# A two-block transformer kernel: the first slot alone, equal tile offsets, norms and bias turns moved, a shorter end

## The chip, the cores and the metric
The kernel runs on one core of one Trainium2 chip. The metric is the device time of one execution in microseconds, as the median of several runs. Engines: TensorE (PE; its weight loads are PEld), VectorE (DVE), ScalarE (ACT), GpSimd (POOL) and SyncE (SP, which only issues DMAs here; ScalarE issues some too).

## The reference, cut to what matters
Input x has 512 tokens of width 1024. Everything is fp32.

Block one: h = rms_norm(x); one projection gives the inputs of four mixers of width 256: a short convolution, a sparse attention of three parts (compressed tokens, selected blocks, a window; `ksw`, `nq0`, `nq1`, `kvc`), a latent attention with rotary parts (`cq`, `ckv`, called mla), and a stick-breaking attention (`sq0` to `sk1`, called sb). Each mixer's output is normed (`y`), then x += y @ w_out, then a feed-forward of width 4096 with a squared relu.

Block two: retention, gated linear attention and sliding-window attention, each projected and gated, merged, projected, normed and added to x; then

```python
h = rmsnorm(x, norm_ffn_pre)
f = (silu(h @ ffn_w_gate) * (h @ ffn_w_up)) @ ffn_w_down
x = x + rmsnorm(f, norm_ffn_post)
```

## The kernel before
**Layout.** Activations lie transposed: 8 chunks (KD) of 128 features by 512 tokens (T). A projection of 128 output features takes one weight slot (128 x 1024). Each fp32 product is made of three fp32r matmuls (`mm3`, L700): with w and x split in a high and a low part, w_hi x_hi + w_hi x_lo + w_lo x_hi. So a projection (`fm`, L803) is 24 matmuls of 512 columns into one of 8 PSUM banks.

**Weight slots.** SyncE loads slots in order into 3 raw buffers (L2066 to L2082). GpSimd makes the high part (L2054) and the low part by a subtraction (L2056), into 3 buffers each, as these are freed by TensorE. From `fg` 0,3 on ScalarE makes the high part. The slots of the compression weights (`cmp`, steps `cmp_up`) are not split; they have three buffers of their own.

**Order.** `plan()` (L71) writes out one list, ORDER, by hand. Each engine walks the same list and does its own part of each step, in this order, with semaphores between. `together` and `quarters` (L82, L91) cut projections in pieces by chunk (`fmk`, L768); `weave` (L119) spreads filler steps among the steps of an attention: `att_scores` (product, row maximum on VectorE L1822, Exp on ScalarE L1380), `att_norm` (L1840 to L1844), `att_turn` (transposes L962, copied out by ScalarE L1392 as att_pt), `att_pv`. A stick-breaking step `sb_scores` makes two score matmuls, then per head Abs, Exp, Ln on ScalarE (L1418 to L1420) and one operation on VectorE (L1894); `sb_exp` sums these by matmuls and takes Exp (L1428).

**Banks.** `take` (L674) hands out the bank that was filled longest ago and waits until it has been evacuated.

**Norms.** A norm step squares chunks on ScalarE (`sq`, L1157), adds them on VectorE (sq_sum, L1502), sums over partitions with a matmul by ones (`ms`, L717), and makes rstd by Ln and Exp on ScalarE (L1170, L1173). n1, the first one, is applied behind the projection (as r_h, when banks are evacuated: L1586 to L1594), so matmuls run on x times the norm's weights: `u` makes its high part on ScalarE (L1213) and low part on VectorE (L1542). The projection that follows y_out is made from four mixers' norms, the last y3 (L203 to L204).

**The start** (L152 to L166): per chunk `u` and `sq`; TensorE waits for both first slots (`kvc`, `ksw`, L773) and runs chunks 0 to 6 of both, the matmul of n1, and chunk 7; then `nq0`, the compression windows (`cmp_x`, L1722 to L1727), the bias tables (L750, copied at L1532), the norm and scaling of ksw (L1734), `nq1` and so on. At these steps ScalarE issues DMAs for constants.

**The bias turns** (L912): 32 matmuls of 31 columns turn the compressed bias (cb_t) by `flip`, in one block, ahead of `cmp_down`. `cmp_scores` has a softmax on VectorE behind it (L1784 to L1805), `cmp_turn` transposes the result.

**The end.** `down2` (L841, 22 hidden chunks in two halves, slots without a gap) makes f: half 0 is copied from the banks to SBUF (L1711), half 1 is added (L1709). Then the norm `fpost`, and per chunk two VectorE operations: f times weight times rstd (L1507), and x plus this (L2021); SyncE writes each chunk out (L2094).

**SBUF.** Tiles are laid out one behind the other (L363 on). Counted from the start of the partition, x_sb, h, w_hi_t, w_lo_t, u2_hi, hid and most of block two start at 128 modulo 256 bytes; ones, ident, sq, sq_sum, rstd_t, tmp, att_l_t, att_pt and u2_lo05 at 0; the constants of block one behind `gates` at 32 or 64. The low parts of norm2's x are u2_lo05 (chunks 0 to 5) and u2_lo67 (6, 7; at 128): both are called u_lo in the trace.

Of the kernel before, what the change touches and what calls it, by code (L numbers as in the profile page):

```python
# [70 lines left out]
def plan():  # L71
# [47 lines left out]
    def weave(main, filler):  # L119

        n = 0
        for i, step in enumerate(main):
            put(step)
            while n < len(filler) and n * len(main) < (i + 1) * len(filler):
                put(filler[n])
                n += 1
        for step in filler[n:]:
            put(step)
# [32 lines left out]
    run([("sq", "ksw", 0), ("cmp_x", 0), F("nq0"), ("cmp_x", 1), ("bias_tables", 0), ("norm", "ksw"),  # L161
         ("nsa_apply", "ksw"), F("nq1"), ("sq", "nq0", 0), U(0, 0), F("cq0"), ("sq", "nq1", 0), ("norm", "nq0"),
         ("nsa_apply", "nq0"), U(0, 1), F("cqr"), ("norm", "nq1"), ("nsa_apply", "nq1"), ("sq", "cq", 0),
# [4 lines left out]
    for h in range(NH):  # L168
# [3 lines left out]
    run([("cmp_bias", 0), ("cmp_down", 0), ("sq", "kcmp", 0), ("mla_v", 0)] + filler[:5] + [("norm", "kcmp"), ("cmp_apply", 0)] +  # L172
        filler[5:10] + [("cmp_scores", 0)] + filler[10:16] + [("cmp_turn", 0)])
    filler = filler[16:]
# [19 lines left out]
    for n in range(4):  # L194
# [9 lines left out]
        [part(3, 6), ("norm", ("y", 3)), ("y_out", 3), part(6, KD)])  # L204
# [72 lines left out]
    for c in range(KD):  # L277
        order.append(("residual", "fpost", c))
# [32 lines left out]
o_ready m_ready gla_v gla_s gla_kd gla_st gla_a gla_done gla_t prod gate_s merged merged_hl q_s swa_s ft lo_t table""".split()  # L311
# [32 lines left out]
def _program(ctx, nc, a, known):  # L344
# [22 lines left out]
    par = sb("par", [P, -(-NPCOL // 32) * 32])  # L367
    ones = sb("ones", [P, P])
# [9 lines left out]
    small = sb("small", [P, 4, 8])  # L378
    r_col = small[:, :, 7]
# [12 lines left out]
    v1 = sa("v1", [P, NT, 396])  # L392
    gates = sa("gates", [P, NT, 12])
    rb = sa("rb", [N_BUCKETS + 1, NH])
# [15 lines left out]
    conv_t = sa("conv_t", [P, 2, 2 + T])  # L410
# [29 lines left out]
    cmp_bias = sn("cmp_bias_t", [P, NT, NH, N_CMP])  # L440
    cmp_t = sn("cmp_t", [P, 256])
# [66 lines left out]
    f_acc = merged  # L508
    hid2 = [si("hid2_hi", [P, HALF2, T], F32R), si("hid2_lo", [P, HALF2, T], F32R)]
    sig2, sig_g = si("sig2", [P, 2, T]), si("sig_g", [P, 2, T])  # L510
    inner.close()
    area.close()

# [157 lines left out]
    def _(pe):  # L671
# [28 lines left out]
        def mm3(out, wh, wl, xh, xl, start, stop):  # L700

            mm(out, wh, xh, start, False)
            mm(out, wh, xl, False, False)
            return mm(out, wl, xh, False, stop)
# [12 lines left out]
        def ms(key, n_src):  # L717
            srcs, parts, cols, one, *_ = norms[key]
            out = take(("ms", key))
# [24 lines left out]
        for step in ORDER:  # L744
            stage = step[0]
            if stage == "bias_tables":
# [3 lines left out]
                for n, (c0, w) in enumerate(TAB):  # L750
                    out = take(("tab", n))
                    fill(("tab", n), mm(out[0:NH, 0:w], rb[:], onehot[:, c0:c0 + w], True, True))
# [15 lines left out]
            elif stage == "fmk":  # L768

                _, names, src, k0, k1 = step  # L770
                for name in names:
                    if k0 == 0:
                        slot_ready(SLOTS[name][0])  # L773
                        take(name)
# [4 lines left out]
                for k, some in blocks:  # L779
                    fresh = src == "h" and ("h_ready", seen_h, k) not in chunks_seen  # L780
                    if fresh:
# [4 lines left out]
                    for name in some:  # L786
# [8 lines left out]
                    if fresh:  # L795
# [45 lines left out]
            elif stage == "down":  # L841
# [4 lines left out]
                out = take(nm)  # L846
                for k in range(nk):
# [4 lines left out]
                    if o == 0:  # L852
# [3 lines left out]
                               k == 0, k == nk - 1)  # L856
                    if k == nk - 1:
# [54 lines left out]
            elif stage == "cmp_bias":  # L912

                out = take("cmp_bias")
                for qt in range(NT):
                    for h in range(NH):
                        last = mm(out[:, (qt * NH + h) * N_CMP:(qt * NH + h + 1) * N_CMP],
# [1376 lines left out]
```

## Time and profile before

| what | value |
|---|---|
| median of 3 runs | 1884.86 us (1883.58 to 1885.2) |
| the profiled execution | 1885.97 us |
| its span, first to last instruction | 1884.1 us |
| mean granted TensorE clock | 0.988 |
| busy: PE, PEld, DVE, ACT, POOL | 1820.3, 1433.4, 834.9, 504.8, 944.6 us |
| HBM read, written | 158.1, 2.1 MB |

Times of rows are microseconds from the span's start. Matmuls are pipelined: one of 512 columns is shown with 0.39 us, but the next begins 0.227 us behind it. The granted clock is a share of 2.4 GHz; 0.50 is 1.2 GHz.

### The profile page before, as it was taken

The numbers are of one execution on the slowest core, as the hardware profiler recorded it, in microseconds if no ns is written. First come the engines' busy times: TensorE is split into PE (matmuls) and PEld (weight loads), VectorE is DVE, ScalarE is ACT, GpSimd is POOL, SyncE is SP. The second block draws the span as 40 slices with busy tenths as digits, with TensorE's granted clock in tenths as the row PEclk, the third lists the DMA queues.
The fourth block names the chain that finished last, engine by engine and source line by source line (L and its number), as shares of the span: only waits on it lengthen the run. The fifth ranks groups of instructions, "written<-read, shape, count | busy, mean of one in ns | idle before, by whom it ended". The sixth has DMA issues, their size and how long they took to land.

```text
span 1884.1 us, 22044 instructions
## 1 busy us (share of the span) xinstructions
PE 1820.3 (97%) x8468; PEld 1433.4 (76%) x8468; DVE 834.9 (44%) x1386; ACT 504.8 (27%) x1003; POOL 944.6 (50%) x510
## 2 busy tenths in 40 slices
PE   7999989999999999999999999999999999999996
PEld 5785556888888887777887888677778778888885
DVE  6418754532022232435103574666655675315433
ACT  3115664221012001222003232555400232222221
POOL 5343131766666665454665555443466554444541
PEclk9999999999999999999999999999999999999998
DMA  5620100332232223122232222212122223223231
GB/s 179 199 80 26 47 23 34 101 101 97 93 101 90 100 91 111 67 79 79 97 101 79 67 79 76 67 63 68 60 90 97 89 79 100 93 98 101 90 101 56
DMA packets 46728, 162.54 MB, mean 86 GB/s; under 512 B 5392, under 2 KB 6736, under 8 KB 46241
## 3 DMA queue, kind: packets, MB, share of 16 engines
q1 hardware_dynamic: 43088, 154.52, 24.3%
q10 hardware_dynamic: 3537, 6.61, 1.2%
q8 instruction: 69, 1.13, 0.2%
q14 instruction: 34, 0.28, 0.0%
HBM read 158.13 MB, written 2.12 MB: 85 GB/s over the span
## 4 chain that ended last, share of the span: by engine, by line
PE 88%; DVE 6%; ACT 3%; issue 2%; POOL 1%; DMA 0%; ACTq 0%; DVEq 0%; POOLq 0%
PE bank L698 87%; PE bank L962 1%; DVE att_l_t L1822 1%; POOL w_lo_t L2056 1%; DVE o_hi L1485 1%; DVE tmp L1507 0%; ACT att_l_t L1380 0%; DVE o_lo L1486 0%; DVE att_l_t L1842 0%; ACT rstd_t L1170 0%; ACT sq L1157 0%; ACT sb_e L1419 0%; ACT rstd_t L1173 0%; ACT att_pt L1392 0%; DMA w_raw<-in_w 0%
## 5 line engine op out<-in xcount | busy, mean ns | idle before, releaser
L2056 POOL TENSOR_TENSOR w_lo_t<-w_raw,w_hi_t 128x1024 fp32r<-128x1024 f32 x276 | 691.7, 2506 | 188.2 <-ACT w_hi_t L1196 170.1
L2054 POOL TENSOR_SCALAR w_hi_t<-w_raw 128x1024 fp32r<-128x1024 f32 x216 | 234.9, 1088 | 683.7 <-PE bank L698 653.3
L698 PE MATMUL bank<-h_hi,w_hi_t 128*128 128x512 f32 x1088 | 445.3, 409 | 23.6 <-POOL w_lo_t L2056 13.9
L698 PE MATMUL bank<-h_hi,w_lo_t 128*128 128x512 f32 x1088 | 428.4, 394 | 0.0
L698 PE MATMUL bank<-h_lo,w_hi_t 128*128 128x512 f32 x1088 | 421.2, 394 | 0.5 <-DVE h_lo L1575 0.5
L698 PEld LDWEIGHTS bank<-h_hi,w_hi_t 128*128 128x128 f32 x1088 | 207.0, 190 | 87.6 <-issue 39.3
L698 PEld LDWEIGHTS bank<-h_lo,w_hi_t 128*128 128x128 f32 x1088 | 206.6, 190 | 47.0 <-issue 2.6
L698 PEld LDWEIGHTS bank<-h_hi,w_lo_t 128*128 128x128 f32 x1088 | 206.9, 190 | 42.4 <-issue 1.0
L698 PE MATMUL bank<-hid_hi,w_lo_t 128*128 128x512 f32 x432 | 168.2, 389 | 0.0
L698 PE MATMUL bank<-hid_lo,w_hi_t 128*128 128x512 f32 x432 | 168.2, 389 | 0.0
L698 PE MATMUL bank<-hid_hi,w_hi_t 128*128 128x512 f32 x432 | 168.2, 389 | 0.0
L1196 ACT ACTIVATE w_hi_t<-w_raw 128x1024 fp32r<-128x1024 f32 x60 | 63.6, 1060 | 219.8 <-PE bank L698 219.8
L698 PE MATMUL bank<-u_lo,w_hi_t 128*128 128x512 f32 x256 | 100.8, 394 | 0.0
L698 PE MATMUL bank<-u_hi,w_hi_t 128*128 128x512 f32 x256 | 100.1, 391 | 0.0
L698 PE MATMUL bank<-u_hi,w_lo_t 128*128 128x512 f32 x256 | 99.5, 389 | 0.0
L698 PEld LDWEIGHTS bank<-hid_hi,w_lo_t 128*128 128x128 f32 x432 | 81.1, 188 | 16.9
L698 PEld LDWEIGHTS bank<-hid_hi,w_hi_t 128*128 128x128 f32 x432 | 81.1, 188 | 16.8
L698 PEld LDWEIGHTS bank<-hid_lo,w_hi_t 128*128 128x128 f32 x432 | 81.1, 188 | 16.7
L698 PE MATMUL bank<-o_hi,w_hi_t 128*128 128x512 f32 x192 | 78.3, 408 | 2.1 <-DVE o_lo L1486 2.1
L1380 ACT ACTIVATE att_l_t<-att_l_t,small 128x256 f32<-128x256 f32 (+3 forms) x112 | 57.3, 512 | 78.3 <-DVE small L1826 47.1
L1261 ACT ACTIVATE r<-r 128x512 f32<-128x512 f32 x32 | 20.3, 633 | 216.2 <-DVE r L1641 216.2
L1641 DVE SCALAR_TENSOR_TENSOR r<-bank,r_h 128x512 f32<-128x512 f32 x32 | 22.1, 692 | 124.6 <-PE bank L698 120.2
(276 smaller groups left out, 2619.8 us busy)
## 6 DMA issues: line engine op xcount, KB each, us to landing
w_raw<-in_w SPq DMA_DIRECT2D x276, 512.0 KB, 3.2
y<-in_w SPq DMA_DIRECT2D x6, 512.0 KB, 6.2
x_sb<-in_x SPq DMA_DIRECT2D x4, 512.0 KB, 7.6
x_sb<-in_x ACTq DMA_DIRECT2D x2, 1024.0 KB, 5.4
out_y<-x_sb SPq DMA_DIRECT2D x8, 256.0 KB, 2.0
u_raw<-in_w SPq DMA_DIRECT2D x2, 512.0 KB, 6.0
toep<-table ACTq DMA_DIRECT2D x4, 256.0 KB
decay<-in_decay SPq DMA_DIRECT2D x1, 1024.0 KB, 4.9
```

The costliest lines, as they stand in the source:

```text
L698: return pe.matmul(out, lhs, rhs, start=start, stop=stop, **kw)
L962: last = pe.transpose(out[:, b * P:(b + 1) * P], att_l[:, att_at[u] % 4, b * P:(b + 1) * P], ident[:])
L1196: act.activation(w_hi[:, RING[i]], w_raw[:, n % RAW], ACT.Copy).then_inc(*did("wa_hi", i))
L1261: chain(act.activation(r1[:, n % 2], r1[:, n % 2], ACT.Square))
L1380: act.activation(L, L, ACT.Exp, bias=sm[:, 1:2], accum_out=sm[:, 2:3]).then_inc(*did("att_exp", u))
L1485: chain(dve.tensor_copy(hi, t))
L1641: dve.scalar_tensor_tensor(out=r1[:, n % 2], in0=ps(name)[:], scalar=0.0, in1=r_h[:], op0=ALU.max, op1=ALU.mult).then_inc(*release(name))
L1822: dve.tensor_tensor_reduce(L, ps(("sc", u))[:, 0:A["w"]], A["bias"], 1.0, -3.0e38, ALU.add, ALU.max, sm[:, 0:1]).then_inc(*release(("sc", u)))
L2054: pool.tensor_scalar(hi, raw, 1.0, 0.0, ALU.mult, ALU.add).then_inc(*did("w_hi", i))
L2056: pool.tensor_tensor(lo, raw, hi.bitcast(F32), ALU.subtract).then_inc(*did("w_lo", i))
```

## The change
What it does, in the order of the list:

- The first slot alone. `u` runs three chunks ahead of `sq`. `kvc` takes the high parts of chunks 0 to 3 (w_hi and w_lo by x_hi) when its own slot is ready, then `ksw` the same, then both the low parts of these chunks, then chunks 4 to 7.
- The norm n1 stands behind the first quarter of `nq0`, and evacuations of `kvc` and `ksw` behind it; the rest of `nq0` before the square of ksw. `cmp` quarter 0,1 goes ahead of the norm of nq0.
- The bias turns are cut by head in four pieces of 8 matmuls; `cmp_down` comes before them, and `mla_qk` of head 1 before `cmp_scores`.
- `weave` holds an `sb_scores` filler back while the step just put is `att_scores` or `att_norm`, once a turn has been made. Worked through, this moves three such fillers in the latent attention behind the next `att_turn` (sb_scores (0,1), (0,0) and (1,3)); nothing in the other two attentions.
- The norm of y3 comes after chunk 3 of the pieces of `wout`, not after 5.
- Chunk 7 of `down2` keeps one bank over both halves, so VectorE does nothing for it; its square is taken from the bank in two halves of 256 columns, and the norm `fpost` is made in two halves.
- The last adds (`last_add`): for chunks 0 to 3 VectorE only multiplies; TensorE adds x and the product in a bank (by ident), ScalarE copies it to x_sb. Chunks 4 to 7 stay on VectorE. Output order 0, 4, 1, 5, 2, 3, 6, 7.
- Tile offsets: `small` moves ahead of `ones`, v1, gates, rb, conv_t get padding, and 16 elements go ahead of cmp_t, so all start at 128 modulo 256.

```diff
-    for c in range(KD):
-        run([("u", "n1", c), ("sq", "n1", c)])
+    for c in range(KD + 3):
+        run([("u", "n1", c)] * (c < KD) + [("sq", "n1", c - 3)] * (c >= 3))
     part, ends = together(("kvc", "ksw"))
-    run([part(0, KD - 1), ("norm", "n1"), part(KD - 1, KD)] + ends)
+    run([("fmk", ("kvc",), "h", 0, 4, "hi"), ("fmk", ("ksw",), "h", 0, 4, "hi"),
+         ("fmk", ("kvc", "ksw"), "h", 0, 4, "lo"), part(4, KD)])
...
-    run([("sq", "ksw", 0), ("cmp_x", 0), F("nq0"), ("cmp_x", 1), ("bias_tables", 0), ("norm", "ksw"),
-         ("nsa_apply", "ksw"), F("nq1"), ("sq", "nq0", 0), U(0, 0), F("cq0"), ("sq", "nq1", 0), ("norm", "nq0"),
-         ("nsa_apply", "nq0"), U(0, 1), F("cqr"), ...
+    nq0 = quarters("nq0")
+    run(nq0[:1] + [("norm", "n1")] + ends + nq0[1:] + [("sq", "ksw", 0), ("cmp_x", 0), ("cmp_x", 1), ("bias_tables", 0), ("norm", "ksw"),
+         ("nsa_apply", "ksw"), F("nq1"), ("sq", "nq0", 0), U(0, 0), F("cq0"), ("sq", "nq1", 0), U(0, 1),
+         ("norm", "nq0"), ("nsa_apply", "nq0"), F("cqr"), ...
...
-    run([("cmp_bias", 0), ("cmp_down", 0), ("sq", "kcmp", 0), ("mla_v", 0)] + filler[:5] + [("norm", "kcmp"), ("cmp_apply", 0)] +
-        filler[5:10] + [("cmp_scores", 0)] + filler[10:16] + [("cmp_turn", 0)])
+    run([("cmp_down", 0), ("sq", "kcmp", 0), ("cmp_bias", 0), ("mla_v", 0)] + filler[:3] + [("norm", "kcmp"),
+        ("cmp_apply", 0), ("cmp_bias", 1)] + filler[3:4] + [("cmp_bias", 2)] + filler[4:8] + [("cmp_bias", 3)] +
+        filler[8:10] + filler[11:13] + [("cmp_scores", 0)] + filler[13:15] + filler[10:11] + [("cmp_turn", 0)])
...
             while n < len(filler) and n * len(main) < (i + 1) * len(filler):
+                if turned and not callable(filler[n]) and filler[n][0] == "sb_scores" and step[0] in ("att_scores", "att_norm"):
+                    break
...
-        [part(3, 6), ("norm", ("y", 3)), ("y_out", 3), part(6, KD)])
+        [part(3, 4), ("norm", ("y", 3)), part(4, 6), ("y_out", 3), part(6, KD)])
...
+            if (key, c) == ("fpost", KD - 1):
+                act.wait_ge(*full(last_f))
+                sq_free(key, c)
+                for hf in range(2):
+                    act.activation(sq[:, sq_use[(key, c)] % 2, halves_t[hf]], ps(last_f)[:, halves_t[hf]], ACT.Square)\
+                       .then_inc(*did("sq_s", key, c, hf))
+                return
...
+            elif stage == "last_add":
+                r = rstd("fpost")
+                for c in range(KD):
+                    t = last_t[c] if c < N_PE else tmp[:, c % 2]
+                    f = f_acc[:, c] if c < KD - 1 else ps(last_f)[:]
...
+                    for part in halves_t if c == 0 else [slice(0, T)]:
+                        if c == 0:
+                            own("rstd", "fpost", halves_t.index(part))
+                        ins = dve.scalar_tensor_tensor(out=t[:, part], in0=f[:, part], scalar=col("fpost", c),
+                                                       in1=r[:, part], op0=ALU.mult, op1=ALU.mult)
+                    if c < N_PE:
+                        ins.then_inc(*did("last_t", c))
+                    else:
+                        chain(ins)
+                        dve.tensor_tensor(x_sb[:, c], x_sb[:, c], t, ALU.add).then_inc(*did("x_ready", "fpost", c))
```

## Rows read from the trace of the kernel before
**Rows 1.** The page: busy us of each engine, share of the span, instructions.
```profile
PE 1820.3 (97%) x8468; PEld 1433.4 (76%) x8468; DVE 834.9 (44%) x1386; ACT 504.8 (27%) x1003; POOL 944.6 (50%) x510
```
**Rows 2.** Stretches: length, busy and count of each engine, granted clock, DMA, GB/s.
```profile
52.20:55.50 3.30, 3.30 (x7) 1.89 (x7) 0.13 (x1) 1.94 (x3) 1.49 (x1) 0.50 0.45 124
127.30:134.10 6.80, 6.80 (x28) 6.29 (x28) 1.10 (x2) 0.61 (x3) 1.49 (x1) 0.50 0.22 77
...
263.90:270.60 6.70, 6.62 (x15) 4.48 (x16) 3.36 (x12) 3.53 (x9) 0.00 (x0) 0.50 0.00 0
321.90:325.20 3.30, 3.30 (x9) 2.55 (x9) 1.37 (x3) 1.24 (x2) 2.15 (x2) 0.50 0.00 0
```
**Rows 3.** Waits of TensorE: for whom, us in total, times, longest.
```profile
PE bank L698 <- ACT att_pt L1392: 8.2, 4, 4.5
...
PE bank L698 <- ACT sq L1157: 4.4, 4, 1.9
```
**Rows 4.** Timeline of the start: start, us, engine, line, operation [idle before].
```profile
6.09 2.34 POOL L2056 TENSOR_TENSOR w_lo_t<-w_raw,w_hi_t 128x1024 fp32r<-128x1024 f32 x1
8.13 0.72 ACT L1213 ACTIVATE h_hi<-x_sb,par 128x512 fp32r<-128x512 f32 x1 [6.14 <-DMA x_sb<-in_x]
...
8.97 3.76 DVE L1542 SCALAR_TENSOR_TENSOR h_lo<-x_sb,par,h_hi 128x512 fp32r<-128x512 f32 x2 [7.25 <-ACT h_hi L1213]
...
9.52 2.66 POOL L2056 TENSOR_TENSOR w_lo_t<-w_raw,w_hi_t 128x1024 fp32r<-128x1024 f32 x1
...
12.44 0.77 PE L698 MATMUL bank<-h_hi,w_hi_t 128*128 128x512 f32 x1 [12.44 <-POOL w_lo_t L2056]
...
14.71 2.87 DVE L1502 TENSOR_TENSOR sq_sum<-sq_sum,sq 128x512 f32<-128x512 f32 x1
...
27.35 0.63 ACT L1173 ACTIVATE r_h<-r_h 128x512 f32<-128x512 f32 x1
```
**Rows 5.** The chain that ended last, 36 to 57: start, us, what.
```profile
44.56 2.55 DVE x_sb L1734
...
51.23 0.64 ACT sq L1157
```
**Rows 6.** Groups of TensorE from 125 to 130.3: busy us, mean ns.
```profile
L698 PE MATMUL bank<-flip,cb_t 31*128 31x31 f32 x32 | 5.1, 321 | 0.0
```
**Rows 7.** Timeline of TensorE around the first attention pair.
```profile
155.39 1.07 PE L698 MATMUL bank<-sq,ones 96*96 96x512 f32 x2 [1.28 <-ACT sq L1157]
158.43 0.93 PE L962 MATMUL bank<-ident,att_l_t 128*128 128x128 f32 x2 [1.97 <-DVE att_l_t L1842]
```
**Rows 8.** Timeline around the longest wait: ScalarE's Abs, the norm of y1.
```profile
258.73 0.57 ACT L1418 ACTIVATE sb_e<-bank 128x512 f32<-128x512 f32 x1
...
272.12 1.13 PE L698 MATMUL bank<-sq_sum,ones 128*128 128x512 f32 x2
```
**Rows 9.** Timeline of the norm of y3.
```profile
311.49 0.69 DVE L1502 TENSOR_TENSOR sq_sum<-sq 128x512 f32<-128x512 f32 x1 [8.15 <-ACT sq L1157]
...
315.91 1.02 PE L698 MATMUL bank<-sq_sum,ones 128*128 128x512 f32 x2
...
319.69 0.50 PE L698 MATMUL bank<-h_hi,w_hi_t 128*128 128x512 f32 x1 [2.76 <-DVE h_hi L1571]
...
320.95 0.49 PE L698 MATMUL bank<-h_lo,w_hi_t 128*128 128x512 f32 x1 [0.53 <-DVE h_lo L1575]
```
**Rows 10.** Tiles u_lo and hid_lo: duration ns min/median/max, first and last start.
```profile
L698 PE MATMUL bank<-u_lo,w_hi_t x256: 389/395/396, 354.3 to 617.6; 128*128 128x512 f32 x128
...
L698 PE MATMUL bank<-hid_lo,w_hi_t x432: 388/389/390, 443.6 to 1865.7; 128*128 128x512 f32 x144
```
**Rows 11.** Timeline of the end.
```profile
1866.40 0.69 DVE L1709 TENSOR_TENSOR merged_t<-bank,merged_t 128x512 f32<-128x512 f32 x1 [5.40 <-PE bank L698]
...
1870.45 0.75 DVE L1507 SCALAR_TENSOR_TENSOR tmp<-merged_t,par,rstd_t 128x512 f32<-128x512 f32 x1 [3.36 <-ACT rstd_t L1173]
...
1880.95 0.69 DVE L2021 TENSOR_TENSOR x_sb<-x_sb,tmp 128x512 f32<-128x512 f32 x1
```

More of the change, by code:

```diff
@@ L276, in plan @@
     order.append(("norm", "fpost"))
-    for c in range(KD):
-        order.append(("residual", "fpost", c))
+    order.append(("last_add", "fpost"))
     return order, slots
@@ L718, in ms @@
             srcs, parts, cols, one, *_ = norms[key]
+            if key == "fpost":
+                outs = [take(("ms", key, hf))[:, 0:T // 2] for hf in range(2)]
+                pe.wait_ge(*after("sq_v", key, KD - 2))
+                for hf in range(2):
+                    mm(outs[hf], one[:], sq_sum[:, halves_t[hf]], True, False)
+                for hf in range(2):
+                    pe.wait_ge(*after("sq_s", key, KD - 1, hf))
+                    fill(("ms", key, hf), mm(outs[hf], one[:], sq[:, sq_use[(key, KD - 1)] % 2, halves_t[hf]],
+                                             False, True))
+                return
             out = take(("ms", key))
@@ L785, in _ @@
                     wsl = slice(k * P, (k + 1) * P)
-                    for name in some:
+                    for name in some if only != ["lo"] else ():
                         i = SLOTS[name][0]
@@ L845, in _ @@
                 nm = (name[0], name[1], o)
-                out = take(nm)
+                both = name[0] == "down2" and o == KD - 1
+                if nm == last_f:
+                    tenants[nm] = tenants[("down2", 0, o)]
+                    out = ps(nm)
+                else:
+                    out = take(nm)
                 for k in range(nk):
@@ L1162, in norm @@
             functions("exp_ln")
+            if key == "fpost":
+                act.wait_ge(*after("rstd_used", ring_order[ring_at[key] - 3]))
+                for hf in range(2):
+                    r_half = rstd(key)[:, halves_t[hf]]
+                    act.wait_ge(*full(("ms", key, hf)))
+                    act.activation(r_half, ps(("ms", key, hf))[:, 0:T // 2], ACT.Ln, scale=scale,
+                                   bias=small[:, EPS_COL[eps], 6:7]).then_inc(*release(("ms", key, hf)))
+                    act.wait_ge(*evacuated(("ms", key, hf)))
+                    act.activation(r_half, r_half, ACT.Exp, scale=-0.5).then_inc(*did("rstd", key, hf))
+                return
             act.wait_ge(*full(("ms", key)))
@@ L1458, in _ @@
                 act.activation(g_ed[:], g_ed[:], ACT.Exp).then_inc(*did("gla_s", "ed", h))
+            elif stage == "last_add":
+                for c in range(N_PE):
+                    act.wait_ge(*full(("last", c)))
+                    act.activation(x_sb[:, c], ps(("last", c))[:], ACT.Copy).then_inc(*did("last_x", c))
             elif stage == "gla_turn":
@@ L1703, in _ @@
                     hidden_low(name[1], HALF1 - 1)
+                if name[0] == "down2" and o == KD - 1:
+                    continue
                 dve.wait_ge(*full(nm))
```

101 lines of the change are left out of this document (65 added, 36 removed).

## The prediction
> **What bounds the kernel now.** I read the page first: TensorE is busy for 97% of the span, the next engine for 50% [rows 1]. The reader should see two things: nothing but TensorE's own instructions can be worth much in the long stages, and an edit that removes no matmul can only win back TensorE's idle time, its time at the lower clock, the few ns by which a matmul is dearer than its neighbours, and what lies behind the last matmul. Then the view by stretches, cut where the granted clock falls: in five short stretches (four stand here) the clock is 0.50, the lower of its two levels, 1.2 instead of 2.4 GHz [rows 2]. TensorE lost half of each, if it had work. Before the first it had stood still for 1.9 us (the longest of its waits on a square) and before the third for 4.5 us (the longest on att_pt) [rows 3]; before the second it ran 31-column matmuls. Then the timelines and the chain around the stalls, part by part.
>
> **Part 1, the start.** Today the first projection matmul starts at 12.44, when the low part of the second weight slot is done (9.52 + 2.66 = 12.18), though the first slot was done at 6.09 + 2.34 = 8.43 and the first high part of x at 8.13 + 0.72 = 8.85 [rows 4]. The change lets `kvc` run alone on high parts of chunks 0 to 3. It starts at about 8.9, 3.5 us earlier. Its 8 matmuls, at some 0.45 us each at the lower clock (7 in 3.30 us [rows 2]), last until 12.5, just when `ksw` is ready: no new wait there. ScalarE now issues the high parts ahead of the squares (0.7 us each), so chunks 1 to 3 come in time. The low parts don't gain: VectorE's run from 8.97 for 3.76 us for two, and a sum took 2.87 us where 0.69 is usual, both beside GpSimd's subtraction [rows 4]. I put the last low part at about 21.7 instead of 23.3, the two projections done at 23.3, a quarter of `nq0` done at 24.7, and the norm's matmuls then, so r_h appears at about 28.0, as today (27.35 + 0.63) [rows 4]. But TensorE has only 18 matmuls of `nq0` behind it instead of 30 (6 of the pair, 24 of `nq0`): it is 3.3 us ahead.
>
> What it meets next is the chain from r_h over VectorE (three copies, two window builds, a memset, four table copies), ScalarE and back, which today ends with the square at 51.9 [rows 5], TensorE 1.9 us idle before it, and the clock low for 3.4 us after [rows 2, 3]. In this chain the change takes the 0.7 us copy of `nq0` off the path (it now fits in a wait for a DMA), and the weight slots are freed earlier, so GpSimd's subtractions move away from VectorE's two-input operations: the key scaling's first half took 2.55 us beside one [rows 5], the second 0.75 (47.13 to 47.88). Worked through, the square of `nq0` comes at about 47.7 instead of 51.23. TensorE, 5.1 us ahead by then (3.3, plus 1.8 of a `cmp` quarter that the new order puts before the norm), reaches the norm at about 48.3 and need not wait. So the part gives the lead, the wait and half of the cold stretch: 3.3 + 1.9 + 1.7 = **6.9 us** (the 1.8 are only moved). Bounds: if the chain moves by nothing beyond 0.7 us and the cold stretch stays, 3.5; if all is as good as its order, 8.5. SyncE's queue keeps its order (slot numbers don't change); its loads wait for freed slots, all earlier, and ScalarE's DMA issues keep theirs.
>
> **Part 2, bias turns in pieces.** The 32 small matmuls take 5.1 us in one block [rows 6], and inside it the clock falls for 6.8 us [rows 2]. Four pieces of eight between projections and full-width products leave no such block. If the cold stretch goes, 3.4 us come back. Against that: three more changes between kinds of matmul at about 0.2 us; and the scores now come after `mla_qk` of head 1, so that TensorE meets `cmp_turn` some 2.6 us before VectorE's softmax chain (5.3 us from scores to probabilities) is through. Today it pays there later: 1.28 us for a square and 1.97 us for the first weights [rows 7]. This stage's exit is set by VectorE, whose list loses only the copy and the rotation before the first scores. I take **0.5 us**; between 2.5 lost (cold stretch stays, wait is new) and 3 gained.
>
> **Part 3, the stick-breaking scores behind the turn.** TensorE's waits on att_pt are 8.2 us in 4, the longest 4.5 [rows 3]. The timeline shows why: ScalarE takes up the two heads' Abs, Exp, Ln at 258.7 [rows 8] and reaches the transposed weights only behind them and a norm; TensorE goes on at 264, cold [rows 2]. The new rule in `weave` moves three of the scores steps behind `att_turn`: the copy then comes at about 258.7. TensorE's next block (2.6 us) is filled in, but ScalarE's work in front of the norm of y1 (3.7 us of Abs, Exp, Ln, a norm of 1.3, two squares, a copy, two exponentials) is not less: that norm moves from 272.12 [rows 8] to about 268. So 4 us, plus 1 us at the first moved step (a wait of 1.2 us of the same kind), and nothing at the third, where TensorE doesn't wait: **5 us**. Bounds 1.5 (ScalarE gives all back) and 7.
>
> **Part 4, the norm of y3** goes two chunks earlier. Today the norm's matmuls run at 315.91; then TensorE waits 2.76 us for its first high part and 0.53 for the low part [rows 9], then runs 3.3 us cold [rows 2]. After the change 18 matmuls (4.1 us) lie behind the norm's matmuls, where from their start to the first high part 3.7 us are needed (319.63 - 315.91): covered. Left are 0.5 us ahead of the norm (the sum is ready at 311.49 + 0.69 = 312.2, TensorE is there at 315.9 - 4.1 - 0.1 = 311.7) and 0.2 for the last low part. 3.3 - 0.7 + 1.7 (half of the cold stretch) = **4.3 us**; bounds 3.0 and 4.8.
>
> **Part 5, offsets.** `small` moves ahead of `ones`, and tiles of the first area are padded, so that all start at the same remainder of 256 bytes as x and the weights. One tile shows what this may be worth: u_lo's matmuls have a median of 395 ns against 389 at best and for the hidden ones [rows 10]. Six of its eight chunks lie in `u2_lo05`, 128 bytes off in this measure, two in `u2_lo67`, which isn't, and the cheap ones are the latter. Start to start it is about 7 ns, for 192 matmuls 1.3 us. VectorE's two-input operations take 0.69 us on tiles of either kind (sq_sum, merged) [rows 9, 11]. I take **1.3 us**; bounds 0 (the cause is another) and 3, if matmuls beside such tiles in the attention stages gain too.
> The Trainium skill (SBUF — State Buffer, "Who interferes with whom") gives a single rule: only the port pair shared by VectorE and GpSimd causes contention. It knows no cost of an offset for TensorE. By that rule the part is worth 0 and the sum is 1.3 us smaller; the row of u_lo speaks against it.
>
> **Part 6, the end.** From the last projection (1866.40) to the first output step are 4.05 us: add, square, ones product, Ln, Exp; then VectorE makes eight pairs of 0.75 and 0.69, 11.2 us, and the last DMA ends the span 2.5 us later [rows 11]. The change accumulates both halves of chunk 7 in one bank, so the add goes; squares read the bank, in halves; rstd comes in halves, the first after about 2.3 us, the second after 3.1. Then VectorE has chunk 0 in two halves, three single multiplies (2.2 us) and four pairs with 1.39 each (5.55): last output at 3.5 + 2.2 + 5.55 = 11.25 us behind the projection, today 15.24 (1881.64). TensorE's ones and adds of x (0.86 us a product, twice that when cold) and ScalarE's four copies are done by about 8 us; SyncE's order 0, 4, 1, 5, 2, 3, 6, 7 queues none behind a later one. **4.0 us**; bounds 3.3 and 4.5. The bank held from `down2` half 0 to the end leaves seven, which a projection of 5.4 us each doesn't need; without that cover each late bank would cost the 0.7 us of a copy.
>
> **Sum:** 6.9 + 0.5 + 5 + 4.3 + 1.3 + 4.0 = 22.0 us. The profiled execution took 1885.97 us (span 1884.1 and 1.9 around it), the median of the runs is 1.1 lower. 1885.97 - 22.0 = 1864.0; against the median 1862.9. I say 1863.2, between the two.
>
> **Rivals.**
> (a) *The stalls move.* TensorE's lead is eaten by the chains of VectorE and ScalarE, which no part shortens: 3.5 (part 1), -1 (part 2), 1.5, 3.3, 0, 4.0 = 11.3 us, 1873.6. For it: from 162 to 325 TensorE often waits on them [rows 3, 7]. Against: the order, not the amount, made the largest waits. 25%.
> (b) *The clock gives more.* All cold stretches of block one go, and the offsets help the attention stages: 8.5 + 3 + 7 + 4.8 + 3 + 4.3 = 30.6, about 1854.5. For it: dense work stands where idle was. 10%.
> (c) *Slower: equal offsets collide.* If the slow remainder is not the odd one but the one that two engines share, the moved tiles (tmp, sq, att) now share it with x and the weights. Price: up to 7 ns on each of some 6,600 projection matmuls, 46 us, so 1863 + 46 = 1909. It decides from 4 ns on (26 us: the 22 gained and 4 more). Against: the hidden ones run at 389 beside VectorE's work on tiles of the same remainder [rows 10]. 2%.
> (d) *It doesn't do what it says:* the offsets do nothing, and the cold stretches around the bias turns and the norm of y3 stay: 1.3 + 3.4 + 1.7 = 6.4 us less, though the other parts hold: about 1869.5. 10%.
> The forecast has 53%.
>
> **Numbers.** The range from 1857 to 1873.5 leaves out most of (b), (c) and the worse half of (a). About 0.2%, 3.8 us, is what a measurement of this kernel can tell from no change; part 6 alone nearly makes that, so faster 0.96, same 0.02, slower 0.02.
>
> **What would show it.** First matmul near 9; r_h near 28; clock full at 52 to 55, at 127 less 7, and around 312 to 318; no wait over 1.5 us on att_pt, with the copies ahead of the Abs; no wait on h_hi at y3; u_lo's median 389 or 390; last DMA issued 11.3 us behind the last projection. It is wrong if TensorE waits long for the square of `nq0`, for `cmp_p`, or for a new ScalarE step in the attention stage, or if projection matmuls are no longer 227 ns apart.

## The result, and the profile after

The changed kernel takes **1874.95 us** (median of 4 runs, 1873.66 to 1876.29), the kernel before beside it 1884.55: a ratio of 0.995, interval 0.9934 to 0.9966, so 9.6 us faster where some 21 were forecast, and above the range. The sign was right; the size was the size of rival (a), 1873.6, though not by its parts.

The page's first part, as [rows 1]; the span is 1874.5 us, 9.6 less than before:
```profile
PE 1826.0 (97%) x8488; PEld 1433.5 (76%) x8488; DVE 826.7 (44%) x1381; ACT 507.0 (27%) x1010; POOL 943.6 (50%) x510
```
TensorE is busy for 5.7 us longer than before: behind the last projection 9.0 instead of 2.1 us, most of it the 7.3 us of identity products of the new end, and ahead of it 1.2 us less. What is missing is seen in the stretches (columns as in [rows 2]):
```profile
134.00:146.10 12.10, 9.90 (x59) 6.43 (x58) 7.54 (x15) 3.15 (x5) 3.40 (x2) 1.00 0.15 51
146.10:159.70 13.60, 10.16 (x36) 5.88 (x36) 9.21 (x36) 5.73 (x18) 0.00 (x0) 0.50 0.00 0
159.70:163.00 3.30, 3.30 (x20) 2.01 (x16) 1.40 (x5) 0.54 (x3) 0.70 (x1) 1.00 0.00 0
268.90:272.40 3.50, 3.50 (x5) 1.25 (x4) 3.43 (x7) 1.32 (x2) 0.00 (x0) 0.51 0.00 0
702.40:709.30 6.90, 6.04 (x14) 4.78 (x15) 6.87 (x14) 0.00 (x0) 0.00 (x0) 0.51 0.33 131
```
The low stretches at 52, in the bias turns and at the norm of y3 [rows 2] are gone, as forecast. In their place stands one of 13.7 us around the first attention steps, where the kernel before had 3.4; TensorE is busy for 10.16 us of it, half of them lost to the clock. With a longer stretch at 702 (6.8 for 3.4) and a new one of 3.4 at 1371, the low stretches ahead of the end sum up to 34 us in both kernels: none of the clock that I counted as won was won in the sum. (Up to 400 us they went from 23.8 to 17.1; behind that they grew from 10.2 to 17.0.)

To find where the time went, take a mark that both traces have: the start of ScalarE's Ln in each norm. The lead of the changed kernel over the one before, in us, by single profiled executions (mk and mq are the latent attention's keys and queries by head, y the mixers' norms, n2 the norm behind the mixers, pre the one at the end of block one, ret 0 the first of retention, fpre the one ahead of the last feed-forward):

| kernel | ckv | mk 0 | mq 1 | mq 3 | y0 | y1 | y2 | n2 | pre | ret 0 | fpre | time, median |
|---|---|---|---|---|---|---|---|---|---|---|---|---|
| (time in before) | 79.59 | 143.67 | 167.34 | 220.04 | 262.34 | 273.28 | 294.00 | 361.26 | 707.90 | 777.76 | 1529.08 | 1884.55 |
| after | 6.6 | 12.0 | 2.8 | 2.3 | -0.8 | 4.0 | 2.3 | 6.2 | 7.5 | 6.2 | 5.5 | 1874.95 |
| e1 the same | 5.9 | 11.2 | 2.6 | 2.1 | -1.0 | 3.9 | 2.2 | 6.0 | 7.2 | 6.0 | 6.5 | 1875.02 |
| e2 part 2 undone | 6.9 | 6.5 | 6.4 | 6.3 | 2.7 | 6.7 | 5.9 | 9.7 | 11.0 | 10.9 | 10.1 | 1872.24 |
| e3 weave undone | 6.6 | 11.9 | 3.6 | 3.1 | 3.6 | 5.2 | 5.2 | 9.0 | 10.2 | 10.2 | 9.9 | 1872.55 |
| e4 y3 undone | 5.8 | 11.1 | 2.7 | 2.1 | -1.0 | 3.6 | 2.2 | 2.2 | 3.5 | 2.6 | 3.3 | 1876.52 |
| e5 both of e2, e3 | 6.6 | 7.8 | 7.4 | 7.4 | 7.3 | 8.9 | 8.8 | 12.6 | 13.9 | 13.9 | 14.0 | 1870.82 |
| e6 pieces, old order | 7.0 | 12.2 | 9.0 | 8.9 | 5.3 | 9.2 | 8.4 | 12.2 | 13.5 | 13.5 | 14.0 | 1871.0 |
| e7 two fillers | 6.7 | 12.0 | 5.3 | 4.6 | -0.6 | 3.3 | 2.5 | 6.3 | 7.6 | 9.2 | 9.5 | 1874.68 |
| e8 offsets undone | 6.6 | 12.2 | 4.0 | 2.9 | -0.2 | 3.7 | 2.9 | 6.7 | 6.7 | 6.7 | 6.8 | 1875.12 |
| e9 e6 without rule | 7.0 | 12.3 | 8.7 | 8.8 | 8.8 | 9.8 | 9.8 | 13.6 | 14.9 | 14.8 | 14.3 | 1868.18 |
| e10 e9, one step held | 6.5 | 11.8 | 8.2 | 8.2 | 3.9 | 8.2 | 7.0 | 10.9 | 12.2 | 11.1 | 11.7 | 1870.11 |
| e11 e9 without part 1 | 0.2 | 5.5 | 1.4 | 1.5 | 1.5 | 2.5 | 2.5 | 6.3 | 7.6 | 7.6 | 7.2 | 1873.17 |
| e13 held behind att_pv | 7.0 | 12.3 | 7.9 | 8.0 | 7.2 | 12.4 | 9.2 | 13.0 | 14.3 | 14.3 | 14.9 | 1867.83 |
| e14 the same, three | 7.0 | 12.3 | 8.7 | 8.7 | 9.3 | 14.6 | 14.2 | 17.8 | 19.1 | 19.0 | 19.5 | 1862.69 |
| e15 e9 again | 5.5 | 10.8 | 6.1 | 5.5 | 5.5 | 6.5 | 6.5 | 10.3 | 11.6 | 11.6 | 11.1 | 1870.05 |

The row "after" has the account: part 1 gives 6.6, part 2 takes 4.4 (to mq 3; the 12 at mk 0 is only its new place, and mq 1 and y0 don't stand at the same point of the order in all kernels either, while mq 3, y1, y2 and what follows do), part 3 nothing (2.3 to 2.3), part 4 3.8, part 5 1.3, two longer low-clock stretches take 1.9, and the end, 4.1 more, brings it to 9.6. The same program's profile differs by 1.5 us at ckv and 3.3 at mq 3 from another execution's (e9 and e15), because its low stretches differ; so a difference under some 3 us between two rows is read only where it is the step from one mark to the next, and one under 2 us between medians of different series not at all (e9 and e15 are 1.87 apart).

**Part 1** is as forecast. The first matmul, forecast for 8.9, and the square of nq0, forecast for 47.7 (TensorE had no wait of 1.9 us left and the clock stayed up):
```profile
8.71 0.77 PE L709 MATMUL bank<-h_hi,w_hi_t 128*128 128x512 f32 x1 [8.71 <-ACT h_hi L1274]
...
48.57 0.63 ACT L1208 ACTIVATE sq<-x_sb 128x512 f32<-128x512 f32 x1 [6.11 <-issue]
```

**Part 2.** TensorE's waits in the changed kernel, from 134 to 167 us (for whom, us in total, times, longest). Before, from 140 to 174, there were 1.28 and 1.97 [rows 7]:
```profile
PE bank L993 <- DVE att_l_t L1911: 3.3, 1, 3.3
PE bank L971 <- DVE cmp_p L1874: 2.4, 1, 2.4
```
And what VectorE does there, from the timeline of the changed kernel:
```profile
141.09 0.74 DVE L1860 TENSOR_TENSOR cmp_p<-bank,cmp_bias_t 128x248 f32<-128x248 f32 x2 [2.07 <-PE bank L709]
...
145.54 0.67 DVE L1874 TENSOR_TENSOR cmp_p<-cmp_p,cmp_s_t 128x496 f32<-128x496 f32 x1
...
149.06 0.68 DVE L1943 TENSOR_TENSOR mq<-mq,rope_c 96x512 f32<-96x512 f32 x1
...
151.41 0.35 DVE L1911 TENSOR_SCALAR att_l_t<-att_l_t,small,gates_t 128x128 f32<-128x128 f32 x1
```
VectorE now stands idle for 2.07 us until the later scores are there, and the rest of its chain, down to the first weights at 151.4, comes behind them.

**Part 3.** TensorE's waits on att_pt fell from 8.2 to 4.4 us and the norm of y1 came at 268.07, as forecast, but a new wait stands before it:
```profile
268.07 1.19 PE L709 MATMUL bank<-sq_sum,ones 128*128 128x512 f32 x2 [2.18 <-DVE sq_sum L1567]
```
ScalarE's waits from 217.78 to 291.66 us, which in the kernel before (220.04 to 294.0) were 6.8 us in 5 on the same tile:
```profile
ACT att_l_t L1441 <- DVE small L1898: 11.7, 7, 2.7
ACT att_pt L1453 <- PE bank L709: 11.2, 6, 3.8
```

**Part 4.** The wait of 2.76 on the high part [rows 9] and its cold stretch are gone. One wait of another kind came, for a weight slot of GpSimd, which TensorE now reaches 4 us sooner:
```profile
320.41 0.50 PE L709 MATMUL bank<-h_hi,w_hi_t 128*128 128x512 f32 x1 [0.99 <-POOL w_lo_t L2142]
```

**Part 5.** u_lo's matmuls, as [rows 10]:
```profile
L709 PE MATMUL bank<-u_lo,w_hi_t x256: 387/389/396, 348.2 to 610.2; 128*128 128x512 f32 x128
```

**Part 6.** The end, as [rows 11]: squares of the bank, Ln of the first half, first output step and last. The last ends at 1872.04, 11.2 us behind the last projection's matmul (1860.47 + 0.39); forecast were 11.25:
```profile
1860.89 0.66 ACT L1199 ACTIVATE sq<-bank 128x256 f32<-128x256 f32 x2 [6.12 <-PE bank L709]
...
1862.25 0.47 ACT L1219 ACTIVATE rstd_t<-bank,small 128x256 f32<-128x256 f32 x1 [0.70 <-PE bank L709]
...
1863.20 0.49 DVE L2088 SCALAR_TENSOR_TENSOR sig<-merged_t,par,rstd_t 128x256 f32<-128x256 f32 x1 [7.70 <-ACT rstd_t L1222]
...
1871.35 0.69 DVE L2094 TENSOR_TENSOR x_sb<-x_sb,tmp 128x512 f32<-128x512 f32 x1
```

### The profile page after: what moved, and what is told of

Read it like the earlier page. It is cut to its first block, busy times and chain, and to the rows that moved or that the text cites. A ratio compares the mean times of both kernels' runs of the same rounds, so it can differ in the third digit from the quotient of the medians.

```text
span 1874.5 us, 22078 instructions
## 1 busy us (share of the span) xinstructions
PE 1826.0 (97%) x8488; PEld 1433.5 (76%) x8488; DVE 826.7 (44%) x1381; ACT 507.0 (27%) x1010; POOL 943.6 (50%) x510
## 4 chain that ended last, share of the span: by engine, by line
PE 89%; DVE 6%; ACT 3%; issue 1%; POOL 1%; DMA 1%; ACTq 0%; SPq 0%; DVEq 0%; POOLq 0%
PE bank L709 87%; PE bank L993 1%; DVE att_l_t L1911 1%; DVE att_l_t L1891 1%; DVE o_hi L1550 0%; POOL w_lo_t L2142 0%; ACT sq L1208 0%; DVE o_lo L1551 0%; DMA x_sb<-in_x 0%; ACT att_l_t L1441 0%; DVE h_lo L1607 0%; ACT sb_e L1480 0%; ACT att_pt L1453 0%; DVE att_l_t L1913 0%; ACT h_hi L1274 0%
```

## The experiments

The theories that the runs tell apart: **A**, parts 2 and 3 cost time, each by itself, and the others hold; its rivals are that an accident of the clock did it, that a chain of VectorE or ScalarE takes back any lead, or that another part failed. Each kernel was timed 4 to 11 times beside the kernel before, in four series (e1 to e4, e5 to e8, e9 to e12, e13 to e15), in which the kernel before took 1883.1 to 1883.8.

**e1: nothing edited.**

> The changed kernel once more, nothing edited, to have it beside the three kernels that follow and to see a second profile. Theory A (its low-clock stretches belong to the order of its instructions): the long one of 13.7 us from 146.1 to 159.7 comes again within 1 us of the same place, and the median is 1875.0 +/- 1. Rival R (where the clock falls is an accident of one execution): this stretch is missing or as short as 3.4 us, and the span differs by some 4 us from the first profile.

1875.02 us (0.9954, 0.9942 to 0.9967). The long stretch came again, but from 149.7, 3.6 us behind its first place where within 1 was expected, and 10.2 us long, so that both end at 159.8 or 159.9; another of 3.4 came at 33.7, where the first profile had none. So the place belongs to the order; the length partly to the execution. All six profiles with the new order of scores (after, e1, e3, e4, e7, e8) have 10.2 or 13.7 us here, all eleven with the old order (before among them) 3.4 or 6.8.

**e2: part 2 undone.**
```
+run([("cmp_bias", h) for h in range(NH)] + [("cmp_down", 0), ("sq", "kcmp", 0), ("mla_v", 0)] + filler[:5] +
+    [("norm", "kcmp"), ("cmp_apply", 0)] + filler[5:10] + [("cmp_scores", 0)] + filler[10:16] + [("cmp_turn", 0)])
+filler = filler[16:]
```

> The changed kernel with the first block's old order: bias turns in one row ahead of the down product, scores before head 1's keys and queries. Theory A (part 2 costs what the stages between 134 and 167 lost: 6.6 us of lead at the turn of cmp_p, 2.8 us after the first attention steps): about 4 us faster than the changed kernel, 1871 us, with the low-clock stretch between 146 and 160 no longer than 7 us, and one of some 7 us inside the bias turns about 6 us earlier than in the kernel before, near 121. Rival B (the lead is lost there whatever the order, because VectorE's chain from the scores to the first weights sets the end of the stage): within 1 us of the changed kernel, 1875, with the milestone behind the first attention steps where the changed kernel has it, at 164.6.

1872.24 us, 2.8 less than e1; by the marks 4.2 at mq 3 and 3.7 at fpre. The cold bias turns are back and yet it is the faster one:
```profile
121.00:127.80 6.80, 6.80 (x27) 6.20 (x27) 1.10 (x2) 1.02 (x3) 1.27 (x1) 0.50 0.22 77
151.70:155.10 3.40, 3.17 (x8) 2.11 (x8) 2.24 (x13) 2.82 (x9) 0.00 (x0) 0.50 0.00 0
```
Part 2 costs 2.8 to 4.2 us. Rival B, that the lead goes there in any order, falls.

**e3: the rule in `weave` undone.**
```
-if turned and not callable(filler[n]) and filler[n][0] == "sb_scores" and step[0] in ("att_scores", "att_norm"):
-    break
```

> The changed kernel without the rule that holds sb_scores back behind a turn. Theory A (part 3 only moves the stall, because ScalarE's list up to the norm of y2 is as long as before): the norm of y1 comes some 4 us later, at about 273, but the norm of y2 stays within 1 us of 291.7 and the time within 1 us of the changed kernel, 1875. Rival B (part 3 has its 5 us, and something else lost them): 1878.5 to 1880.

1872.55 us, 2.5 less than e1; both expectations missed. The stall of 4.5 us on att_pt is back, and y2 is 3.0 us earlier. So part 3 doesn't move its gain, it costs. (Of the 3.0, 1.0 stands at mq 3 already, ahead of the first moved step: from mq 3 to y2 this kernel gains 2.1 us, the changed one 0.1.)

**e4: the norm of y3 where it was.** `[part(3, 6), ("norm", ("y", 3)), ("y_out", 3), part(6, KD)]`

> The changed kernel with the norm of y3 where it was, behind six chunks of the last three projections. Theory A (part 4 is worth what the milestones behind it show, 3.8 us): 1878.8 us, with TensorE waiting 2.8 us for the first high part again. Rival B (it is worth its wait alone and the rest was the accident of the clock there): 1877.3.

1876.52 us, 1.5 more than e1 and less than either expected, though the marks part by 3.8 at n2 and 3.2 at fpre. The wait of 2.75 us and a stretch of 3.4 at 320.0 are back. The step from y2 to n2 is 3.6 to 3.8 us in all 14 profiles with the part and 0.0 in the three without it (before, e4, e12); the median shows less of it than this, and why, the runs don't say.

**e5: parts 2 and 3 undone together** (e2's and e3's edits).

> The changed kernel with the first block's old order and without the weave rule, parts 1, 4, 5 and 6 kept. Theory A (each of the two parts costs by itself, part 2 2.8 us and part 3 2.5 us by the medians of the runs so far): the sum of both, 1869.7 us, with the norm of y2 7.3 to 9.4 us earlier than in the kernel before. Rival B (the two share one stall, so that either undoing is enough): no better than the better of them, 1872.

1870.82 us (1867.72 to 1872.27), 4.2 less than e1, where the sum of both would be 5.3 and one alone 2.8: a little nearer the sum. By the marks it is the sum (6.6 at y2, of 3.7 and 3.0), but its profiled execution, 1867.78, was 3.0 below its median.

**e6: the pieces kept, the old order of scores and rotation.**
```
-    filler[8:10] + filler[11:13] + [("cmp_scores", 0)] + filler[13:15] + filler[10:11] + [("cmp_turn", 0)])
-filler = filler[15:]
+    filler[8:10] + [("cmp_scores", 0)] + filler[10:16] + [("cmp_turn", 0)])
+filler = filler[16:]
```

> The changed kernel with its bias turns in pieces, but the scores again before head 1's keys and queries and its rotation before the turn of cmp_p; weave rule kept. Theory A1 (what costs in part 2 is the new order, which brings TensorE to cmp_turn and to the first weights before VectorE's chain; the pieces are harmless or help): at or below the run with part 2 wholly undone, 1869 to 1872.5 us, with no wait over 1 us before cmp_turn. Rival A2 (the pieces are what costs; VectorE or ScalarE gets the bias table or the slots too late): 1875 us, as the changed kernel.

1871.0 us, 4.0 below e1. This splits part 2: pieces with the old order lead by 8.9 at mq 3, the block with the old order by 6.3 (e2; 7.4 in e5, whose stretch in the block was 3.4 us instead of 6.8), pieces with the new order by 2.1. By these rows alone the pieces would be worth +1.5 to 2.6 us and the new order -6.8; but this profile is of the fastest of six executions, 3.2 below their median. The step from ckv to mq 3 over all profiles says it better: pieces with the old order 0.1 to 1.9 us in seven (e6, e9, e10, e11, e13, e14, e15; mean 1.3), the block with the old order -0.6 to 0.8 in four (before, e2, e5, e12; mean 0.0), pieces with the new order -3.5 to -4.4 in five (after, e1, e3, e4, e8; mean -3.8). So the new order costs **some 5 us** (4.0 by e6's median beside e1's), clear of the spread, and the pieces bring **about 1.3**, which is not. From 121 to 134, through the last three of the pieces (the first is at 119, the clock full there too), the granted clock is full:
```profile
121.00:134.00 13.00, 13.00 (x60) 8.72 (x59) 3.10 (x6) 4.77 (x9) 1.20 (x1) 1.00 0.14 45
```

**e7: two quarters of a projection into the two waits.** One quarter before `cmp_turn`, the next ahead of head 1's rotation (`filler[13:15] + filler[18:19] + filler[10:11]`, then `filler[19:20] + filler[15:18] + filler[20:]`).

> The changed kernel with two more quarters of the conv projection in the two waits of part 2: one ahead of cmp_turn, the next ahead of head 1's rotation (which then no longer stands before the first weights in VectorE's queue). Theory A1 (TensorE waits there because its order has nothing to do; work moved in is work gained): the wait of 2.4 us before cmp_turn goes, the one of 3.3 before the first weights falls to under 2, the clock does not stay low for 10 us or more, and the time is 1870 to 1872 us. Rival B (VectorE's chain sets the exit of the stage; filling in only moves the waits behind it): within 1 us of the changed kernel, 1875.

1874.68 us: Rival B by the time. The waits did shrink, 5.6 us to 4.2 in five, but TensorE turned the first weights at 150.96 (151.81 in after), and the low stretch is again 10.2 us. The profile leads by 4.6 at mq 3, 2.3 more than after, and has 2.5 at y2, as after; between them stands a low stretch of 3.4 us more, at 254.2. In the old order the first weights are turned at 149.34 (e9), because VectorE has the scores 2.9 us sooner (0.4 of it that execution's lead at ckv):
```profile
138.18 0.74 DVE L1858 TENSOR_TENSOR cmp_p<-bank,cmp_bias_t 128x248 f32<-128x248 f32 x2 [0.24 <-PE bank L707]
...
147.69 0.29 DVE L1889 CUSTOM_DVE_ANT_0 att_l_t<-bank,toep 128x128 f32<-128x128 f32 x1
```
Filling TensorE's wait gave no gain that the median shows; whether the 2.3 us up to mq 3 were real and lost again to the clock, one profile doesn't tell.

**e8: every tile back in its place** (`small` behind `u2_lo05`, no padding).

> The changed kernel with every tile where it was before the offsets were made equal. Theory A (the 128 bytes cost TensorE some 7 ns for each of 192 matmuls whose moving operand lies there): u_lo's median back at 394 to 395 ns, 1.3 us slower than the changed kernel, 1876.3. Rival B (what moved u_lo was its neighbours in time, not the place): its median stays at 389 and the time at 1875.0.

```profile
L708 PE MATMUL bank<-u_lo,w_hi_t x256: 389/395/396, 347.6 to 610.9; 128*128 128x512 f32 x128
```
The median is back at 395, and the step in lead between n2 and pre, 1.3 in all 14 profiles with equal offsets, is 0.0 here, as in e12. In both, 193 of the 256 matmuls take 393 ns or more and 63 less, which fits the six chunks in `u2_lo05` and the two in `u2_lo67`; in the changed kernel one of 256 does. So the cause is the place of the tile (this run moves all of them back at once, but within it dear and cheap ones run side by side). The time, 1875.12, is that of e1 all the same: e8's low stretch at 704 was 3.4 us, e1's 6.8. A gain of 1.3 us is below what the medians tell apart; the mark and the tile's row show it.

**e9: e6's and e3's edits together.**

> The changed kernel with the pieces kept but the old order of scores and rotation, and the weave rule gone. Theory A (pieces help by the clock, the new order and the rule cost): the lead of the pieces run at the end of the first attention, 8.9 us, plus the 1.5 us that the kernel without the rule gains between there and the norm of y2: that norm 10.3 us earlier than before, time 1868 to 1869 us, under both kernels and at least 1.5 below the run with parts 2 and 3 undone. Rival (run to run, the clock takes back what a lead wins): 1870.5 to 1871, as the runs with either.

**1868.18 us** (0.9918, 0.9904 to 0.9931), under both kernels. y2 came 9.8 earlier, expected were 10.3.

**e10: the same, with the rule left for one step**, `filler[n] == ("sb_scores", 0, 0)`.

> The same, with the weave rule left for one step alone, sb_scores of pair 0, tile 0. Theory C (by the matmuls' starts the rule's first moved step costs 2.3 us, the second gains 3.8 and the third costs 1.7): att_pt's wait of 4.5 us goes, no wait of 2.2 us on sq_sum takes its place, and the norm of y2 comes 1 to 2 us earlier than in the kernel just above; time 1866.5 to 1868. Rival D (ScalarE has as much to do before the norm of y2 in any order, so that what the second step gains is given back behind it): within 1 us of the kernel above, its norm of y2 within 0.7.

1870.11 us: both expectations missed, and y2 is 2.7 us later than in e9. But now the cause stands alone. ScalarE and TensorE in e10's timeline:
```profile
250.39 0.19 ACT L1441 ACTIVATION_READ_ACCUMULATOR att_l_t<-att_l_t,small 128x1 f32 x1
254.51 0.45 ACT L1453 ACTIVATE att_pt<-bank 128x128 f32<-128x128 f32 x2 [3.93 <-PE bank L709]
254.84 0.60 ACT L1479 ACTIVATE sb_e<-bank 128x512 f32<-128x512 f32 x1
```
```profile
249.19 1.16 PE L709 MATMUL bank<-x_sb 64*128 64x512 f32 x2 [0.92 <-DVE small L1891]
250.28 1.22 PE L709 MATMUL bank<-sbm,ident 128*128 128x128 f32 x4
251.29 1.91 PE L709 MATMUL bank<-sq_sum,ones 128*128 128x512 f32 x2
253.14 1.28 PE L709 MATMUL bank<-att_pt,mv 128*64 128x128 f32 x16
```
The copy of the transposed weights now heads ScalarE's queue, but it can't start before `att_pv` of the pair before has read att_pt, and in TensorE's order that `att_pv` stands behind the scores, their masks and the norm of y0. ScalarE is idle for 3.93 us. In e9 it does its 3.7 us of Abs, Exp and Ln from 249.91 to 253.61, just then.

**e11: e9 without part 1** (start and first block's order as before).

> The first kernel of this row with the start and the norm-and-sparse-attention chain as before the change (part 1 undone). Theory A (part 1 is worth what its milestone shows, 6.6 us at the norm of cq): 6 to 7 us above it, 1875, with the square of nq0 waited for 1.9 us at 50 and the clock low there. Rival B (the lead is eaten later by VectorE's chain in the attention stages): 3 to 4 us above it.

1873.17 us: part 1 is worth 5.0 us by the medians, between the two expectations. By the marks 6.8 at ckv, 7.3 at mq 3 and 7.2 at fpre, so beside e9 nothing of it is eaten on the way (beside e15, the same kernel as e9 with one low stretch more and one longer, it is 5.3, 4.0 and 3.9, and 3.1 by medians of two series); it has its wait of 2.0 us and this stretch:
```profile
52.00:55.40 3.40, 3.40 (x7) 2.02 (x7) 0.17 (x1) 1.95 (x3) 1.50 (x1) 0.50 0.38 119
```

**e12: the new end alone**, every other part undone.

> The kernel before with the new end alone. Theory A: 4.0 us faster than before (3.3 to 4.5), 1879.8 against 1883.8, with 12.2 to 12.3 us from the last norm's Ln to the end of the span, where there were 15.0, and 1.3 from the add of the last chunk. Rival B (the held bank makes projections of the last stage wait and takes part of it): 2 to 3 us.

1879.54 us (11 runs) against 1883.22: 3.7 us, 0.9981 (0.9972 to 0.9989). From the last Ln to the end of the span 12.2 us, before 15.0. Theory A; up to fpre its marks are within 0.25 us of the kernel before, so the held bank costs nothing that shows.

**e13: the held step behind `att_pv` too.** The rule of e10 with `step[0] in ("att_scores", "att_norm", "att_turn")`.

> The best kernel so far with sb_scores of pair 0, tile 0, and so the norm of y0 behind it, held back past att_turn and past att_pv of the pair before. Theory E (the rule costs because ScalarE's copy then heads its queue while TensorE's att_pv, which frees att_pt, stands behind the scores and the norm: ScalarE idle 3.9 us): with att_pv ahead ScalarE's wait at this place is under 1.5 us, no wait of 4.5 us on att_pt, the norm of y2 1.5 to 3 us earlier than in the best kernel, time 1865 to 1867. Rival D (ScalarE's work up to the norm of y2 sets the pace in any order): the norm of y2 within 0.7 us of the best kernel's, time 1868 +/- 1.

1867.83 us, 2.2 below e15 of the same series, 0.4 below e9. The stage itself decides, from mq 3 on: to y1 the lead grows by 4.5 us (e9: 1.0; e10: 0.0), but of that 3.2 are lost again up to y2, so that over the stage it grows by 1.2 (e9: 1.0; e10: -1.2). So against e10 the place of `att_pv` is worth 2.4 us; against e9 one place alone gains nothing yet, as Rival D says: the next sb_scores step stands ahead of its turn as before, and there is a wait of 2.6 us on sq_sum.

**e14: the same at all three places** where a step of sb_scores would come ahead of `att_turn`.
```
-step[0] in ("att_scores", "att_norm")
+step[0] in ("att_scores", "att_norm", "att_turn")
```

> The same at every place where a sb_scores step would stand ahead of att_turn (three of them). Theory E: at least as good as with one, since the first and third place lost 2.3 and 1.7 us by the same wait: norm of y2 2 to 4 us earlier than in the best kernel, 1864 to 1866.5. Rival D: as the best kernel, or worse by up to 2 where TensorE has nothing to do in place of the moved scores.

**1862.69 us** (1861.9 to 1866.46; 0.9894, 0.988 to 0.9907), 7.4 below e15 of the same series, 5.5 below e9, and some 12 below the changed kernel. ScalarE's wait on att_pt from 211 to 285, and TensorE's over the whole span:
```profile
ACT att_pt L1453 <- PE bank L709: 5.4, 5, 1.7
```
```profile
PE bank L709 <- ACT att_pt L1453: 2.6, 2, 1.3
```
The stretch from mq 3 to y2, first of e9, then of e14 (same columns as [rows 2]):
```profile
211.24:284.25 73.01, 63.80 (x381) 43.02 (x382) 41.14 (x116) 47.00 (x122) 15.21 (x12) 0.95 0.11 37
```
```profile
211.33:279.79 68.46, 61.05 (x379) 41.95 (x380) 40.58 (x116) 46.71 (x121) 15.45 (x12) 1.00 0.12 39
```
ScalarE's work is the same; 4.5 us less pass. 2.75 of them are TensorE's busy time, as no low stretch is left where e9 has one of 6.8 us, and 1.8 its idle time. Rival D falls: the work up to y2 doesn't set the pace, the order does.

**e15: e9 again, beside e13 and e14.**

> The best kernel so far once more, on the same chip as the two above: 1868.2 +/- 1 by every theory, its att_pt wait of 4.5 us at the same place.

1870.05 us (0.9927, 0.9913 to 0.9943; e9 had 0.9918): 0.9 outside the expectation. Its profile has 3.4 us of low clock at 34.3 and 6.8 instead of 3.4 at 150.4.

## Why the prediction missed

**Part 1, right.** 6.9 forecast; 6.6 by the mark, 5.0 by e11's median. The steps (first matmul at 8.7, r_h where it was, the wait at 50 and its stretch gone) stand in the trace; the square was 0.9 us later than forecast, at no cost (the first half of the key scaling still took 1.95 us, 2.55 before, where the second half took 0.75). One thing was not foreseen: in three of the 14 profiles with the new start (e1, e4, e15), and in none of the three with the old one, the clock falls for 3.4 us at 33 to 34, behind the eight small matmuls of the bias tables and with no wait before; these three have 5.5 to 5.9 at ckv, the others 6.5 to 7.0.

**Part 2, wrong: 0.5 forecast, -4.4 measured** (e2: -2.8 to -4.2), below my lower bound of -2.5. The pieces did what was said: the cold stretch went; 3.4 less 0.6 was the working, about 1.3 the step to mq 3, within the spread. The step that failed is "the scores now come after `mla_qk` of head 1, so that TensorE meets `cmp_turn` some 2.6 us before VectorE's softmax chain (5.3 us from scores to probabilities) is through. Today it pays there later". I counted the delay as TensorE's wait, paid once, and wrote in the next sentence that this stage's exit is set by VectorE. If VectorE sets it, scores that come 2.9 us later move the exit by that; its idle 2.07 before `cmp_p` shows it. And TensorE's waits grew from 3.3 to 5.6 us in a place that pays in clock: 13.7 or 10.2 us low instead of 3.4. That the two come together and undo a part was no term of mine: some -5 for the order in all. How much of it is the delay and how much the clock, no run separates cleanly. An estimate from the step to mq 3: of the seven kernels with pieces and old order, those with 6.8 us of low clock (e11, e13, e15) stand 1.0 us behind those with 3.4, so 10.2 instead of 3.4 would be some 2 of the 5 us, and the delay the other 3.

**Part 3, wrong in sign: 5 forecast, 0.1 in the account, and -2.5 by e3.** The step that failed is "the copy then comes at about 258.7". It took the copy as ready as soon as it was ahead in ScalarE's order. What the copy waits for is the buffer, and the one who frees it, `att_pv` of the pair before, was now itself behind the moved steps in TensorE's order. ScalarE's idle time on this tile went from 6.8 to 11.2 us. That "TensorE's next block (2.6 us) is filled in" and that ScalarE's work "is not less" was right, and y1 came at 268.07, but I then let the lead at y1 stand for the lead of the stage; at y2 it was gone. The zero for the third moved step ("TensorE doesn't wait") was a guess from TensorE's side alone. e10 shows the wait alone, and e14 takes it away: the same rule, one kind of step later, gains 4.5 us of the stage (5.5 to 7.4 by the medians) where the rule as it was made costs 1.4 to 2.0 from mq 3 to y2 (after and e1 beside e3, e2 beside e5, e6 beside e9) and 2.5 by e3's median. So the 5 us were there to be had, and this change didn't have them.

**Part 4, right:** 4.3 forecast, 3.8 by the marks in every profile that has the part, 1.5 by e4's median. Not foreseen: TensorE, sooner there, meets GpSimd's weight slot (0.99 us).

**Part 5, right:** 1.3 and 1.3. The Trainium skill (SBUF — State Buffer, "Who interferes with whom") has only the port pair of VectorE and GpSimd as a cause of contention, and going by it the part was worth nothing; e8 shows that the place of the tile moves TensorE's matmuls by 6 ns. Whether that is contention between engines at all, no run shows.

**Part 6, right:** 4.0 forecast; 4.1 in the account, 3.7 alone (e12).

**The clock elsewhere, no term:** stretches of 6.8 instead of 3.4 at 702 and a new one at 1371 took 1.9 us from the profiled execution, and other executions have them elsewhere. The kernel before had two of its own behind 400 us, 3.4 us at 711 and 6.8 at 1499, which the prediction's five leave out. Rival (c) is out, and so is rival (d): the offsets gave their 1.3, and both stretches that it let stand went; what came was a new one. Rival (a) had the time, in part by luck: it had the place of the loss ("TensorE's lead is eaten by the chains of VectorE and ScalarE") and -1 for part 2, but 1.5 for part 3, and lost 3.4 of part 1, which held.

## What to carry to other kernels

Before moving a step behind another, ask for the first instruction that then heads each engine's queue what frees its input and its output buffer, and where that instruction now stands in its own engine's order: here a copy was put first whose buffer a later matmul had to free. Where a stage's exit belongs to one engine, judge every reordering by when that engine's inputs come; work put into the other engine's wait (e7) brought no gain in the median. And judge a part by the mark at the end of its stage (y2), not by the first one behind the edit (y1).

## What the runs showed of the hardware

A matmul of 512 columns takes 395 ns instead of 389, and 234 instead of 227 from start to start, if its moving tile begins 128 bytes off modulo 256 from the others; with the tiles back in their old places (e8) it is 395 again. The clock falls again and again in the same places, after the same waits, but for 3.4 us in one execution and 6.8 in another of the same program (e9 and e15 at 150), and 10.2 or 13.7 (e1 and after); e9 and e15, which differ in nothing else, are 1.5 us apart at ckv and 3.3 at mq 3, more than some parts of the change are worth. With another order it can vanish: e14's whole first block after 154 us is at the full clock.
